# Forgetting attention in two passes: high and low halves of the queries stacked, keys held twice, values side by side

## The chip, the cores and the metric

The kernel runs on one core of a Trainium2 chip. The metric is the device time of one execution in microseconds. TensorE multiplies, with the stationary operand loaded by its own instruction; ScalarE, VectorE and GpSimd do the elementwise work; SyncE and ScalarE issue DMAs here.

## The reference, cut to what matters

A decoder layer of four sub-layers for 512 tokens of width 1024: a SwiGLU, a mixer (forgetting attention with 8 heads of 64 beside gated linear attention), a cross-attention to 256 memory tokens, and a second SwiGLU. All is float32. The part that the change touches:

```python
def fox_attention(q, k, v, log_f):
    c = jnp.cumsum(log_f, axis=1).transpose(0, 2, 1)
    ...
        s = jnp.einsum('bhqd,bhkd->bhqk', qi, kt).astype(jnp.float32) * scale
        s = s + ci[..., None] - c[:, :, None, :]
        s = jnp.where(k_pos[None, :] <= q_pos[:, None], s, -jnp.inf)
        p = jax.nn.softmax(s, axis=-1).astype(vt.dtype)
        return jnp.einsum('bhqk,bhkd->bhqd', p, vt)
```

with 8 heads, 64 wide, and queries taken in blocks of 128.

## The kernel before

Float32 products are made from float32r parts. Each operand x is kept as a rounded high part (ScalarE, a copy into float32r) and a low part, x minus high (VectorE, or GpSimd for the weights), and a product is three passes of TensorE: high by high, low by high, high by low (`three`).

Weights stream in blocks of 128x1024 through four slots. SyncE fetches a block in two pieces of 256 KB (`fetch`, L493), ScalarE rounds it into w_hi (`round_block`, L644), GpSimd subtracts it into w_lo (`split`, L588), TensorE uses it and frees the slot. The order on every engine is written out by hand; each engine works its own queue in order, and semaphores tie the queues together.

**The mixer's projections** take four blocks each: queries (group 0), keys (1), values (2), and then the linear attention's groups 3 to 5. `in_evacuate` takes a group out of the banks. For queries and keys VectorE scales a bank into tmp (L1282, one row block m holds two heads of 64 rows), ScalarE rounds, VectorE subtracts. A head's queries lie in their own head slot of q_hi and q_lo, 64 rows of them, and the other 64 rows of the slot are zero: `three` contracts over 128 rows, two heads of keys, and the zero rows drop the head that is not wanted. GpSimd clears those rows once (L626), in its queue between the low halves of the mixer's third and fourth block. Keys are kept two heads to a row block (k_hi_a, k_hi_b, k_lo), values with all heads beside each other (v_hi, v_lo).

ScalarE's order from the keys to the heads' loop is: round keys of heads 0 to 3 (`in_evacuate(1, (0, 1))`), a weight block, the first decays, a weight block, `cum_spread(0)` (which needs TensorE's `cum_rows(0)`, L1678, made right ahead of the last value block), the second decays, keys of heads 4 to 7, values of the first two token blocks, a weight block, the other values, and then the loop. TensorE's wait ahead of the loop is for the low halves of queries and keys and for the clearing.

**The loop over heads** (`fox_attention` on each engine) has 32 units, 8 heads by 4 query blocks. For a unit k TensorE makes the mask product (L1701) and the three score products (`scores`), then `fill(k)`, one or two quarters of a block of groups 3 to 5 as the table FILL says, then, for the third unit after a head's last, the head's output (`output`), and then the transposes of unit k-2 (`turn`, L1713). VectorE takes maxima (L1165) and normalises; ScalarE takes exponentials (L851) and rounds the transposed probabilities (pt_hi, L861), and VectorE makes their low half (pt_lo, L1178). The output product has 128 columns of values, two heads, as stationary operand, so half of the rows of bank 3 are not used. ScalarE rounds the head's 64 rows into fox_hi (L842), and VectorE subtracts into fox_lo (L1152). Behind the loop comes `gla`, where TensorE waits for the last of these, runs a warm-up product (L1445), and then the first scores of the linear attention, which wait for ScalarE's two copies of the turned keys (L916).

## Time and profile before

| | us |
|---|---|
| median of 3 runs | 1189.07 (1186.98 to 1190.51) |
| the profiled execution | 1188.42 |
| its span | 1186.7 |
| TensorE busy in the span | 1160.1 |
| mean granted clock | 0.998 |

A span runs from the first to the last instruction of the profiled execution. The time of that execution is 1.7 us more than its span, for what lies around it. Matmuls are pipelined: the duration that is printed for one of them overlaps the next, so what a product costs is read from where the next one starts. The mixer's projections begin at about 375 us, the loop over heads runs from 452.7 to about 571.7 us.

### The profile page before, as it was taken

Reading aid. Unit: us, or ns where it says so; the run is one execution under the profiler, and the core shown is the slowest. Engines: PE = TensorE matmul, PEld = TensorE weight load, DVE = VectorE, ACT = ScalarE, POOL = GpSimd, SP = SyncE. Lnnn points to the kernel's source line nnn. Section 1 sums busy time; section 2 is a strip of 40 time slices with the busy share of each in tenths; the row PEclk is TensorE's granted clock in tenths of the full one; section 3 lists DMA queues with packets and bytes.
Section 4 is the critical chain, followed back from the end, with each engine's and each line's share of the span. In section 5 each row is a group of like instructions: output and inputs, shape, how many; then the busy total and the mean of one; then the engine's idle time right before and its main releaser. Section 6 shows DMA issues by size and latency. Waiting matters only on the chain.

```text
span 1186.7 us, 15254 instructions
## 1 busy us (share of the span) xinstructions
PE 1160.1 (98%) x5664; PEld 965.5 (81%) x5664; DVE 352.4 (30%) x718; ACT 454.6 (38%) x744; POOL 499.4 (42%) x227
## 2 busy tenths in 40 slices
PE   8999999999999999999899999899999999999998
PEld 7888888888888778787778988778888888888886
DVE  2221311310006274655545204544122131130003
ACT  6232332322126455454535545456423233231213
POOL 5354354354443542222325754256434435435441
PEclk9999999999999999999999999999999999999999
DMA  6323333332322222111223442233332333323232
GB/s 201 105 91 99 96 94 101 92 103 89 106 89 71 89 89 72 54 54 43 83 69 109 160 142 89 73 126 107 104 105 90 98 96 92 103 89 106 89 107 107
DMA packets 86141, 115.13 MB, mean 97 GB/s; under 512 B 8974, under 2 KB 54092, under 8 KB 86092
## 3 DMA queue, kind: packets, MB, share of 16 engines
q1 hardware_dynamic: 86000, 114.44, 29.7%
q8 instruction: 33, 0.54, 0.2%
q14 instruction: 16, 0.13, 0.0%
q10 hardware_dynamic: 92, 0.02, 0.0%
HBM read 112.34 MB, written 2.10 MB: 96 GB/s over the span
## 4 chain that ended last, share of the span: by engine, by line
PE 61%; issue 24%; POOL 11%; DVE 2%; DMA 1%; ACT 1%; POOLq 0%; SPq 0%; DVEq 0%
PE bank L1436 20%; PE bank L1440 20%; PE bank L1437 20%; POOL w_lo L588 10%; PE bank L1477 1%; DVE h L1073 1%; DMA raw<-in_ffn_w_gu 1%; DVE bank L1062 0%; PE bank L1513 0%; POOL q_hi L626 0%; POOL q_lo L626 0%; DVE tmp L1062 0%; DVE f_ms L1060 0%; ACT w_hi L644 0%; ACT xh L658 0%
## 5 line engine op out<-in xcount | busy, mean ns | idle before, releaser
L588 POOL TENSOR_TENSOR w_lo<-raw,w_hi 128x1024 fp32r<-128x1024 f32 x204 | 488.3, 2403 | 665.0 <-ACT w_hi L644 664.3
L1436 PE MATMUL bank<-xh,w_hi 128*128 128x512 f32 (+1 forms) x912 | 349.8, 384 | 2.7 <-POOL w_lo L588 2.0
L1437 PE MATMUL bank<-xh,w_lo 128*128 128x512 f32 (+1 forms) x912 | 348.3, 382 | 0.0
L1440 PE MATMUL bank<-xl,w_hi 128*128 128x512 f32 (+1 forms) x912 | 348.3, 382 | 0.0
L644 ACT ACTIVATE w_hi<-raw 128x1024 fp32r<-128x1024 f32 x204 | 213.3, 1057 | 349.5 <-DMA raw<-in_ffn_w_down 167.5
L1436 PEld LDWEIGHTS bank<-xh,w_hi 128*128 128x128 f32 x912 | 171.5, 188 | 36.6 <-POOL w_lo L588 2.6
L1440 PEld LDWEIGHTS bank<-xl,w_hi 128*128 128x128 f32 x912 | 171.4, 188 | 33.6
L1437 PEld LDWEIGHTS bank<-xh,w_lo 128*128 128x128 f32 x912 | 171.5, 188 | 32.0
L1436 PE MATMUL bank<-w_hi,mid_hi 128*128 128x512 f32 x352 | 137.3, 390 | 0.0
L1440 PE MATMUL bank<-w_lo,mid_hi 128*128 128x512 f32 x352 | 137.0, 389 | 0.0
L1437 PE MATMUL bank<-w_hi,mid_lo 128*128 128x512 f32 x352 | 136.9, 389 | 0.0
L1107 DVE TENSOR_TENSOR tmp<-bank,rinv 128x512 f32<-128x512 f32 x44 | 30.2, 686 | 343.8 <-PE bank L1440 327.6
L753 ACT ACTIVATE tmp<-tmp 128x512 f32<-128x512 f32 x44 | 27.8, 633 | 152.0 <-DVE tmp L1107 152.0
L1436 PEld LDWEIGHTS bank<-w_hi,mid_hi 128*128 128x128 f32 x352 | 66.1, 188 | 14.1 <-DVE tmp L1108 0.6
L1440 PEld LDWEIGHTS bank<-w_lo,mid_hi 128*128 128x128 f32 x352 | 66.1, 188 | 13.9
L1437 PEld LDWEIGHTS bank<-w_hi,mid_lo 128*128 128x128 f32 x352 | 66.1, 188 | 13.6
L1436 PE MATMUL bank<-w_hi,xh 128*128 128x512 f32 x160 | 64.6, 404 | 3.3 <-POOL w_lo L588 2.9
L1440 PE MATMUL bank<-w_lo,xh 128*128 128x512 f32 x160 | 63.0, 394 | 0.0
L1437 PE MATMUL bank<-w_hi,xl 128*128 128x512 f32 x160 | 63.0, 394 | 0.0
L1062 DVE SCALAR_TENSOR_TENSOR bank<-bank,g_row 128x512 f32<-128x512 f32 x20 | 13.7, 693 | 135.4 <-ACT sq L691 135.4
L1062 DVE SCALAR_TENSOR_TENSOR tmp<-bank,g_row 128x512 f32<-128x512 f32 x12 | 8.1, 684 | 105.8 <-ACT sq L691 105.8
L1436 PEld LDWEIGHTS bank<-w_hi,xh 128*128 128x128 f32 x160 | 30.5, 190 | 10.4 <-issue 4.1
(232 smaller groups left out, 1211.6 us busy)
## 6 DMA issues: line engine op xcount, KB each, us to landing
raw<-in_ffn_w_gu SPq DMA_DIRECT2D x176, 256.0 KB, 2.9
raw<-in_ffn_w_down SPq DMA_DIRECT2D x88, 256.0 KB, 2.8
raw<-in_mix_w_in SPq DMA_DIRECT2D x48, 256.0 KB, 2.8
raw<-in_mem_w_kv SPq DMA_DIRECT2D x32, 256.0 KB, 3.1
raw<-in_mem_w_o SPq DMA_DIRECT2D x32, 256.0 KB, 2.9
raw<-in_mix_w_out SPq DMA_DIRECT2D x16, 256.0 KB, 3.0
raw<-in_mem_w_q SPq DMA_DIRECT2D x16, 256.0 KB, 2.9
h<-in_x SPq DMA_DIRECT2D x4, 512.0 KB, 5.3
```

The lines of the kernel that those rows point to most:

```text
L588: gp.tensor_tensor(w_lo[:, n % SLOTS, :], raw[:, n % SLOTS, :], w_hi[:, n % SLOTS, :].bitcast(F32), ALU.subtract).then_inc(lo_ready, 1)
L644: act.activation(w_hi[:, n % SLOTS, :], raw[:, n % SLOTS, :], ACT.Copy).then_inc(hi_ready, 1)
L753: act.activation(tmp[:, pair, :], tmp[:, pair, :], ACT.Silu).then_inc(silu_done, 1)
L1062: dve.scalar_tensor_tensor(out=weighted_at(n)[:, :], in0=out_bank(s, n)[:, :], scalar=POST_SCALE[s], in1=g_row[:, cols], op0=ALU.mult, op1 ...
L1073: dve.scalar_tensor_tensor(out=h[:, t, cols], in0=weighted_at(n)[:, :], scalar=f_rinv[:, r], in1=h[:, t, cols], op0=ALU.mult, op1=ALU.add) ...
L1107: dve.tensor_tensor(tmp[:, pair, :], b[pair][:, :], rinv[:, :], ALU.mult).then_inc(gate_scaled, 1)
L1436: pe.matmul(dst, w[0], x[0], start=start, stop=False, skip_group_check=loose)
L1437: pe.matmul(dst, w[1], x[0], start=False, stop=False, skip_group_check=loose)
L1440: return pe.matmul(dst, w[0], x[1], start=False, stop=stop, skip_group_check=loose)
L1477: last = pe.matmul(bank[m][:, TOK[half]], slot[:, cols], x[:, c, TOK[half]], start=half == c == 0 and not low_w and not low_x, stop=False, ...
```

## The change

The queries of a head are stacked along the contraction: the head's slot of q_hl has its high part in its own 64 rows and its low part in the other 64. The keys of each head are held twice, once in each half of the rows, so that one pass with k_hi gives high by high and low by high, and a pass with k_lo gives high by low and also low by low. The second copy of the keys is made by DMA, from one half of the rows to the other, 8 for k_hi and 8 for k_lo, issued by ScalarE. Of the values of a head the high and the low part lie side by side as 128 stationary columns (v_hl), so that two passes, with pt_hi and pt_lo, fill both halves of bank 3: one with the product of the high part, one with that of the low part. ScalarE copies one half out, VectorE adds the other, and high and low part of the sum are made one unit later. The clearing of the q tiles is gone. The diff, cut:

```diff
-            gp.wait_ge(w_used, B_IN)
-            gp.wait_ge(lo_ready, B_IN + 3)
-            for n, t in enumerate((q_hi, q_lo)):
-                for e in range(2):
...
-                    gp.memset(heads[:, :, e, :].bitcast(F32), 0.0).then_inc(q_zero, 1)
@@ ScalarE, in_evacuate @@
                     elif g == 1:
                         act.wait_ge(in_tmp, 4 + m + 1)
-                        act.activation(key_hi(m), tmp[:, m, :], ACT.Copy).then_inc(in_hi, 1)
+                        for e, done in enumerate((k_even_hi, in_hi)):
+                            r = head_rows(e)
+                            act.activation(k_hi[r, 2 * m + e, :], tmp[r, m, :], ACT.Copy).then_inc(done, 1)
+                        for e, (done, count) in enumerate(((k_even_hi, m + 1), (in_hi, 4 + m + 1))):
+                            act.wait_ge(done, count)
+                            act.dma_start(k_hi[head_rows(e + 1), 2 * m + e, :].bitcast(F32),
+                                          k_hi[head_rows(e), 2 * m + e, :].bitcast(F32))\
+                               .then_inc(k_hi_twin[m // 2], 16)
...
+            def low_twins(half):
+
+                for m in (2 * half, 2 * half + 1):
+                    for e, (done, count) in enumerate(((k_even_lo, m + 1), (in_lo, 4 + m + 1 + 4 * half))):
+                        act.wait_ge(done, count)
+                        dst = key_lo(2 * m + e)
+                        act.dma_start(dst[head_rows(e + 1), :].bitcast(F32),
+                                      dst[head_rows(e), :].bitcast(F32)).then_inc(k_lo_twin[half], 16)
@@ ScalarE, fox_attention @@
-                    r = slice(FOX_D * (hd % 2), FOX_D * (hd % 2 + 1))
-                    act.activation(fox_hi[r, hd // 2, :], bank[3][r, :], ACT.Copy).then_inc(y_h, 1)
+                    r, other = fox_rows_of(hd), fox_rows_of(hd + 1)
+                    act.activation(fox_y[r, hd // 2, :], bank[3][other, :], ACT.Copy).then_inc(y_part, 1)
+
+                def round_rows(done):
...
+                    act.wait_ge(y_sum, hd + 1)
+                    act.activation(fox_hi[r, hd // 2, :], fox_y[r, hd // 2, :], ACT.Copy).then_inc(y_h, 1)
 
                 for k in range(N_FOX + LATE + 2):
+                    if k == 4:
+                        low_twins(1)
...
                     output(k - LATE - 1)
+                    round_rows(k - LATE - 2)
@@ ScalarE, mixer @@
                 in_evacuate(2, (0, 1))
+                low_twins(0)
                 round_to(B_IN + KB * 3 + 2)
@@ VectorE, fox_attention @@
+                    dve.wait_ge(y_part, hd + 1)
+                    dve.tensor_tensor(fox_y[r, c, :], bank[3][r, :], fox_y[r, c, :],
+                                      ALU.add).then_inc(y_sum, 1)
+
+                def low_rows(done):
...
                     dve.wait_ge(y_h, hd + 1)
-                    dve.tensor_tensor(fox_lo[r, c, :], bank[3][r, :], fox_hi[r, c, :].bitcast(F32),
+                    dve.tensor_tensor(fox_lo[r, c, :], fox_y[r, c, :], fox_hi[r, c, :].bitcast(F32),
                                       ALU.subtract).then_inc(y_l, 1)
@@ TensorE, scores @@
-                        pe.wait_ge(in_lo, 12)
+                        pe.wait_ge(k_hi_twin[1], 16 * 4)
+                        pe.wait_ge(k_lo_twin[1], 16 * 4)
...
-                    three(dst, (q_hi[:, hd, tok], q_lo[:, hd, tok]), (key_hi(c)[:, 0:w], k_lo[:, c, 0:w]),
-                          False, True, True).then_inc(scored, 1)
+                    pe.matmul(dst, q_hl[:, hd, tok], k_hi[:, hd, 0:w], start=False, stop=False, skip_group_check=True)
+                    pe.matmul(dst, q_hl[:, hd, tok], key_lo(hd)[:, 0:w], start=False, stop=True,
+                              skip_group_check=True).then_inc(scored, 1)
@@ TensorE, output @@
-                        last = three(bank[3][:, q0:SEQ],
-                                     (v_hi[:, j, c * P:(c + 1) * P], v_lo[:, j, c * P:(c + 1) * P]),
-                                     (pt_hi[:, j, q0:SEQ], pt_lo[:, j, q0:SEQ]), j == 0, j == TC - 1, True)
+                        q0 = min(j, 2) * P
+                        for pt in (pt_hi, pt_lo):
+                            last = pe.matmul(bank[3][:, q0:SEQ], v_hl[:, j, hd, :], pt[:, j, q0:SEQ],
+                                             start=j == 0 and pt is pt_hi, stop=j == TC - 1 and pt is pt_lo,
+                                             skip_group_check=True)
@@ TensorE, mixer @@
-                pe.wait_ge(in_lo, 6)
+                pe.wait_ge(in_lo, 4)
                 pe.wait_ge(q_even_lo, 4)
-                pe.wait_ge(q_zero, 4)
+                pe.wait_ge(k_hi_twin[0], 16 * 4)
+                pe.wait_ge(k_lo_twin[0], 16 * 4)
                 fox_attention()
```

ScalarE's queue before, from the second decays (L818, L819) to the first exponential of the loop. Here k_hi_b is the keys of heads 4 to 7, and the w_hi row is a weight block.

```order
L831 ACTIVATE cum_b<-bank 128x512 [waits cb_done]
L818 ACTIVATE gke<-gke 128x1024
L819 ACTIVATE gk<-gb 128x1024
L805 ACTIVATE k_hi_b<-tmp 128x512 [waits in_tmp,exps]
L805 ACTIVATE k_hi_b<-tmp 128x512 [waits in_tmp]
L809 ACTIVATE v_hi<-bank,rinv_tok 128x512 [waits hinv,pair_done] x2
L644 ACTIVATE w_hi<-raw 128x1024 [waits landed3]
L809 ACTIVATE v_hi<-bank,rinv_tok 128x512 [waits hinv,w_used] x2
```

The same stretch of ScalarE's queue with the change, from the keys of heads 4 to 7 to the weight block.

```order
L817 ACTIVATE k_hi<-tmp 64x512 [waits in_tmp,exps]
L817 ACTIVATE k_hi<-tmp 64x512
L820 DMA k_hi<-k_hi 64x512 [waits k_even_hi]
L820 DMA k_hi<-k_hi 64x512 [waits in_hi]
L817 ACTIVATE k_hi<-tmp 64x512 [waits in_tmp]
L817 ACTIVATE k_hi<-tmp 64x512
L820 DMA k_hi<-k_hi 64x512 [waits k_even_hi]
L820 DMA k_hi<-k_hi 64x512 [waits in_hi]
L829 ACTIVATE v_hl<-bank,rinv_tok 128x8x64 [waits hinv,pair_done] x2
L840 DMA k_lo_a<-k_lo_a 64x512 [waits k_even_lo]
L840 DMA k_lo_a<-k_lo_a 64x512 [waits in_lo]
```

Two further DMAs, for the low keys of heads 2 and 3, follow there. Two operations on keys became four with four DMAs, each DMA behind a wait for the operation that made its source; the same happened to the keys of heads 0 to 3 earlier in the queue. The four DMAs of low keys stand ahead of the weight block and of the loop.

TensorE's queue before, at the first two units of the loop; the mask product is L1701.

```order
L1701 MATMUL bank<-causal,ident_r 128x256 [waits q_zero,q_even_lo,in_lo]
L1436 MATMUL bank<-k_hi_a,q_hi 128x256
L1437 MATMUL bank<-k_hi_a,q_lo 128x256
L1440 MATMUL bank<-k_lo,q_hi 128x256
L1701 MATMUL bank<-causal,ident_r 128x256 [waits cb_ready]
```

TensorE's queue with the change, at the same place.

```order
L1759 MATMUL bank<-causal,ident_r 128x256 [waits k_hi_twin0,k_lo_twin0,q_even_lo,in_lo]
L1762 MATMUL bank<-k_hi,q_hl 128x256
L1763 MATMUL bank<-k_lo_a,q_hl 128x256
L1759 MATMUL bank<-causal,ident_r 128x256 [waits cb_ready]
L1762 MATMUL bank<-k_hi,q_hl 128x256
```

One score product per unit is gone, and the first mask product waits for the keys' copies in place of the clearing.

## Rows read from the trace of the kernel before

**Rows 1.** The page's first part: busy time, share of the span, instructions of TensorE.

```profile
PE 1160.1 (98%) x5664; PEld 965.5 (81%) x5664; DVE 352.4 (30%) x718; ACT 454.6 (38%) x744; POOL 499.4 (42%) x227
```

**Rows 2.** Timeline of TensorE in the loop: start, us, engine, line, operation.

```profile
506.67 0.28 PE L1436 MATMUL bank<-k_hi_b,q_hi 128*128 128x256 f32 x1
506.79 0.28 PE L1437 MATMUL bank<-k_hi_b,q_lo 128*128 128x256 f32 x1
506.90 0.28 PE L1440 MATMUL bank<-k_lo,q_hi 128*128 128x256 f32 x1
...
515.01 0.39 PE L1436 MATMUL bank<-pt_hi,v_hi 128*128 128x512 f32 x1
515.23 0.39 PE L1437 MATMUL bank<-pt_hi,v_lo 128*128 128x512 f32 x1
515.46 0.39 PE L1440 MATMUL bank<-pt_lo,v_hi 128*128 128x512 f32 x1
```

**Rows 3.** Timeline at the mixer's fourth weight block, GpSimd and TensorE.

```profile
384.84 3.66 POOL L626 MEMSET q_hi<- 64x2048 f32 x2
388.56 3.67 POOL L626 MEMSET q_lo<- 64x2048 f32 x2
...
394.75 0.50 PE L1436 MATMUL bank<-xh,w_hi 128*128 128x512 f32 x1 [1.11 <-POOL w_lo L588]
```

**Rows 4.** Timeline from the first keys to the loop's first product.

```profile
441.00 1.23 ACT L805 ACTIVATE k_hi_a<-tmp 128x512 fp32r<-128x512 f32 x2 [7.01 <-DVE tmp L1282]
...
442.13 1.05 ACT L644 ACTIVATE w_hi<-raw 128x1024 fp32r<-128x1024 f32 x1
...
447.03 0.40 PE L1678 MATMUL bank<-cum_hl,sel 128*128 128x512 f32 x1
447.22 0.80 SPq L493 DMA_DIRECT2D raw<-in_mix_w_in  x2
...
447.46 0.60 ACT L831 ACTIVATE cum_b<-bank 128x512 f32<-128x512 f32 x1 [0.84 <-PE bank L1678]
...
449.98 1.15 ACT L805 ACTIVATE k_hi_b<-tmp 128x512 fp32r<-128x512 f32 x2
...
451.04 1.25 ACT L809 ACTIVATE v_hi<-bank,rinv_tok 128x512 fp32r<-128x512 f32 x2
...
452.18 1.05 ACT L644 ACTIVATE w_hi<-raw 128x1024 fp32r<-128x1024 f32 x1
...
452.71 0.28 PE L1701 MATMUL bank<-causal,ident_r 128*128 128x256 f32 x1
```

**Rows 5.** Operations of 64 rows on a q tile: count, min/median/max ns, first and last start.

```profile
L802 ACT ACTIVATE q_hi<-tmp x8: 629/631/633, 409.7 to 414.3; 64x512 fp32r<-64x512 f32 x8
...
L1152 DVE TENSOR_TENSOR q_lo<-bank,q_hi x8: 682/688/695, 473.5 to 572.5; 64x512 fp32r<-64x512 f32 x8
```

**Rows 6.** DMA issues: count, KB each, median us from issue to landing.

```profile
raw<-in_mix_w_in SPq DMA_DIRECT2D x48, 256.0 KB, 2.8
...
out<-h SPq DMA_DIRECT2D x8, 256.0 KB, 2.0
```

**Rows 7.** Waits from 370 to 640 us: us in total, times, longest us.

```profile
DVE pt_lo L1178 <- ACT pt_hi L861: 46.1, 26, 3.5
...
PE bank L1713 <- DVE pt_lo L1178: 2.5, 4, 1.0
...
PE bank L1436 <- DVE pt_lo L1178: 2.0, 2, 1.4
```

**Rows 8.** Timeline behind the last head.

```profile
572.53 1.09 ACT L916 ACTIVATE gla_a<-bank 128x512 f32<-128x512 f32 x2
...
574.35 0.72 PE L1839 MATMUL bank<-gq,gk 64*128 64x128 f32 x8
```

**Rows 9.** Windows: PE, PEld, DVE, ACT, POOL busy, then granted clock, DMA share, GB/s.

```profile
746.00:748.00 2.00, 0.38 (x3) 0.38 (x4) 0.86 (x2) 1.11 (x2) 1.09 (x1) 1.00 0.00 0
750.00:752.50 2.50, 2.50 (x8) 1.95 (x7) 0.69 (x1) 0.59 (x3) 0.00 (x0) 0.50 0.00 0
```

**Rows 10.** Timeline of TensorE inside and behind that dip.

```profile
750.06 0.63 PE L1440 MATMUL bank<-w_lo,xh 128*128 128x512 f32 x1
750.49 0.63 PE L1436 MATMUL bank<-w_hi,xh 128*128 128x512 f32 x1
...
753.04 0.39 PE L1436 MATMUL bank<-w_hi,xh 128*128 128x512 f32 x1
753.27 0.39 PE L1437 MATMUL bank<-w_hi,xl 128*128 128x512 f32 x1
```

More of the change, by code:

```diff
@@ L284, in build @@
         reset = sb("reset", [P, SEQ], at=shared + 100 * kib)
-        fox_hi, fox_lo = (t[:, :, :].rearrange("p (c e) n -> p c e n", e=2)[:, :, 0, :] for t in (q_hi, q_lo))
+        fox_hi, fox_lo = (t[:, :, :].rearrange("p (c e) n -> p c e n", e=2)[:, :, 0, :] for t in (q_hl, k_hi))
+        q_flat = sb("q_flat", [P, FOX_H, SEQ], at=shared + 16 * kib)
+        fox_y = q_flat[:, :, :].rearrange("p (c e) n -> p c e n", e=2)[:, :, 0, :]
         gla_o = sb("gla_o", [P, GLA_H, 2, SEQ], at=shared)
@@ L357, in build @@
         in_tmp = sem("in_tmp")
-        q_zero = sem("q_zero")
+        k_even_hi = sem("k_even_hi")
+        k_even_lo = sem("k_even_lo")
+        k_hi_twin = [sem(f"k_hi_twin{i}") for i in range(2)]
+        k_lo_twin = [sem(f"k_lo_twin{i}") for i in range(2)]
         q_even_hi = sem("q_even_hi")
@@ L376, in build @@
         y_l = sem("y_l")
+        y_part = sem("y_part")
+        y_sum = sem("y_sum")
         ke_turned = sem("ke_turned")
@@ L446, in wait_group, with fox_rows_of, head_rows, key_lo @@
                 eng.wait_ge(w_used, B_IN + KB * (g + 1))
-        def key_hi(c):
-            return (k_hi_a, k_hi_b)[c // 2][:, c % 2, :]
+        def fox_rows_of(hd):
+            return slice(FOX_D * (hd % 2), FOX_D * (hd % 2 + 1))
+        def head_rows(e):
+            return slice(FOX_D * (e % 2), FOX_D * (e % 2 + 1))
+        def key_lo(hd):
+            if hd < 2:
+                return k_lo_a[:, hd, :]
+            return k_lo_b[:, hd - 2, :] if hd < 6 else k_lo_c[:, hd - 6, :]
         def fox_slot(u):
@@ L1182, in fox_attention @@
                     output(k - LATE - 1)
+                    low_rows(k - LATE - 2)
                     for g in (3, 5):
```

66 lines of the change are left out of this document (39 added, 27 removed).

## The prediction

> **What bounds the kernel now.** I began with the page's busy shares. TensorE is busy for 98% of the span [rows 1], so this change is priced in TensorE time first: by the time between the starts of two products, since the printed durations of one product overlap the next. In the heads' stage a 512-column product follows the last after 0.23 us, a 256-column one after 0.12 us [rows 2]; taking 0.17 us for 384 columns is the value between them. Then I looked, stretch by stretch, for places where TensorE waits although the share says 98%, because there work taken from TensorE may come back as a longer wait. There are three kinds. Before the mixer's fourth weight block TensorE waits 1.11 us for GpSimd, which has just been clearing the q tiles [rows 3]. Inside the heads' stage it waits for VectorE's low halves, in ones and twos of a microsecond. At the stage's start it does not wait at all today: the first product of the heads starts at 452.71 [rows 4], right behind the last value product. That last place is where I expect the change to be decided, since all that the heads now need is made there by ScalarE.
>
> **Part 1: products removed.** A unit's scores were three products after the mask, and are two. The moving widths of a head's four units are 256, 256, 384 and 512, so one product fewer per unit saves 0.12 + 0.12 + 0.17 + 0.23 = 0.64 us a head. The output was three products for each of four key blocks (512, 384, 256 and 256 columns) and is two: 0.64 us again. Over 8 heads that is 16 x 0.64 = 10.2 us [rows 2]. All of it lies on TensorE's own queue. Where VectorE already holds TensorE up, part may be lost; I book that in part 4. The pitch of the 256-column products is not held up by the weight load, or 256 columns would not take half of what 512 take.
>
> **Part 2: the clearing of the q tiles goes.** GpSimd cleared four half tiles from 384.84 to 392.23 (3.66 and 3.67 us for two each), then made the low half of the fourth block, and TensorE waited 1.11 us for it [rows 3]. With the clearing gone that low half can start as soon as ScalarE has rounded the block, more than two microseconds earlier, and nothing else is late there: -1.1 us.
>
> **Part 3: the keys' copies delay the first scores.** TensorE now waits, before its first score, for four copies of k_hi and four of k_lo. Follow ScalarE's queue, in the times of the profile before. (a) Keys of heads 0 to 3: two operations of 128 rows started at 441.00, and the next operation at 442.13 [rows 4], 1.13 us. Now there are four of 64 rows, and 64 rows cost as much as 128: 0.63 us each [rows 5]. After each pair ScalarE waits for its own end and then issues two DMAs. The nearest price of an issue is SyncE's, 0.80 us for two pieces [rows 4]. So a pair costs about 1.3 + 0.8 = 2.1 us and both 4.1 us, 3.0 us more than before. (b) What follows is unchanged and was nearly back to back: cum_b started at 447.46 after 0.84 us of idle time, so 3.0 - 0.84 = 2.1 us arrive there. (c) Keys of heads 4 to 7: started at 449.98, now 452.1, and again 4.1 us instead of 1.06: 456.2. (d) The two v_hi operations, 1.14 us by their starts [rows 4]: 457.4. (e) Four more issues at 0.4 us: the last one starts at 458.6. (f) Its landing. No SBUF to SBUF copy is in this trace. The nearest rows are the output pieces, 256 KB in 2.0 us, and the weight pieces, 256 KB in 2.8 us [rows 6]; a copy here is 64 rows x 2 KB = 128 KB and reads no HBM, so I take 2.0 with some queueing, 2.3. TensorE starts at 460.9 instead of 452.7: +8.2 us. Ends: 5.5 us (issues as cheap as nothing, landing 2.0) and 9.5 us (landing 2.8, waits between the pairs). A second stall lies inside this one and costs nothing more: the block rounded at 442.13 comes 3.0 us later, its low half ends at about 449 where TensorE wants it at 447.3, but TensorE then only reaches the same wait later.
>
> By the Trainium skill (DMA: Bandwidth & Descriptors, Rules for kernel authors) transfers to disjoint partition halves serialize, since both use the same engines. The copies are such halves; their ScalarE issues are spaced 0.4 us apart anyway, so by that rule the sum would move by less than the range of (f). No row here shows two of them together.
>
> **Part 4: more work for ScalarE and VectorE in the heads' loop.** Each head's output was one ScalarE copy (rounding) and one VectorE subtraction. Now ScalarE copies the other half out of the bank, VectorE adds, ScalarE rounds one unit later, VectorE subtracts: one 64-row operation more on each, 0.63 and 0.69 us [rows 5]. VectorE's stands, in its queue, before the maximum of the next head's first unit, and TensorE's transposes are behind that. Further, the low keys of heads 4 to 7 are four 64-row subtractions instead of two of 128 rows (+1.4 us on VectorE at unit 2), and ScalarE issues four DMAs before the exponential of unit 4 (+1.6 us there). If all of it reached TensorE it would be 7 x 0.69 + 1.4 + 1.6 = 7.8 us, if none 0. Most of it is covered: in the mixer VectorE stood idle 46.1 us before its low halves of the probabilities, waiting for ScalarE, and TensorE waited for those low halves only 4.5 us in six places [rows 7], four of them (2.5 us) before the transposes. I price the added operation in full at those four and halve it, since VectorE has idle time of its own beside them: 4 x 0.69 / 2 = 1.4 us, and 0.7 us for units 2 to 4: +2.1 us, ends 0 and 6.
>
> **Part 5: the way into the linear attention.** ScalarE's two copies of the turned keys follow the last head's output. They started at 572.53 and took 1.09 us; TensorE's first score product there was at 574.35, with the copies done at 573.6 [rows 8]. Now VectorE's addition (0.69) and ScalarE's rounding (0.63) come first, so the copies end at about 575.0: +0.7 us, ends 0 and 1.4. TensorE's own wait ahead of its warm-up products keeps its length, as it now waits for the addition where it waited for the subtraction.
>
> **Part 6: the clock.** The trace holds one dip: after a stretch of 2 us in which TensorE was busy 0.38 us, the granted clock read 0.50 (1.2 GHz) [rows 9], and 512-column products followed each other after 0.43 us instead of 0.23 [rows 10]; some seven products were hit, about 1.6 us. The stall of part 3 is an idle stretch of some 7 us, far longer than the one before that dip, so I expect another dip whose end lies in the first scores: +1.6 us, ends 0 and 3.4 (if it lasts over twice as many products). By the Trainium skill (TensorE: Matmul & The Clock Gate, the part on the HAM clock gate) the array falls to 1.2 GHz when idle and only sustained activity brings it back. The row agrees with that (0.50 right behind the idle stretch), and the rule speaks against this change: by it the sum below holds at +1.3 us, and if one dip in a whole execution were chance it would be -0.3 us.
>
> **The sum.** -10.2 - 1.1 + 8.2 + 2.1 + 0.7 + 1.6 = +1.3 us, against the profiled execution's 1188.4 us (span 1186.7): 1189.7. The median of the runs is 0.65 us above that execution, which gives **1190.4 us**. A measurement of this kernel can tell about 0.3%, or 3.6 us, from no change, so the forecast is "within 0.3%".
>
> **The rivals.** *A: the copies are in time.* If issuing and landing cost next to nothing on the way, or ScalarE's chain has slack that I don't see, the stall of part 3 stays under 2 us and brings no dip: -10.2 - 1.1 + 1.5 + 2.1 + 0.7 = -7.0, or 1182. For it: nothing but the cheapness of small DMA issues. Against it: ScalarE stands in line from 447.46 on with no gap [rows 4]. Chance 0.17, with the milder forms (a stall of 4 us, 1185) in it. *B, slower: the clock.* The stall splits TensorE's work, the clock stays at 1.2 GHz through the stall and twice as long behind it (3.3 us), and falls a second time at the longer pause of part 5 (1.6 us). The point from which it decides is a clock still at 0.50 well behind the first scores, when the low stretch covers over some ten 512-column products. With the loop's 2.1 us grown to 3.5: 1.3 + 1.7 + 1.6 + 1.4 = +6.0, or 1195. For it: one dip behind 2 us of near idleness. Against it: VectorE and ScalarE get ahead while TensorE runs slowly, which shortens later waits. Chance 0.33 for a time over 1192.6, all mixtures counted. *C: the products don't shrink as planned*, since a stage limited by VectorE's and ScalarE's loop gives nothing back when TensorE gets faster: part 1 shrinks to some 7 us, +4.5, or 1193.6; TensorE's long busy stretches in the stage speak against it. It is in B's chance with 0.08.
>
> **How the numbers follow.** Forecast (within 0.3%) 0.48; faster 0.19 (A, and a little for a part 3 at its lower end); slower 0.33. The range takes in A's milder part and B: 1183.5 to 1196. A full A (1182) and both B and C together lie outside.
>
> **What the changed profile would show.** Part 1: 512-column products at 0.23 us with two per unit, and a heads' stage about 10 us shorter in TensorE products. Part 2: no wait on GpSimd before the fourth block. Part 3: TensorE idle for about 7 us ahead of the first mask product, released by a DMA into k_lo, with ScalarE's queue full in the 12 us ahead. Part 6: a granted clock of 0.50 right behind it. I would be wrong if that stall is under 4 us (then faster), if TensorE's waits for low halves in the loop more than double, or if copies land in over 3 us.

## The result and the profile after

| | before | after |
|---|---|---|
| median, us | 1188.83 (5 runs, 1186.98 to 1190.51) | 1200.49 (5 runs, 1199.59 to 1201.25) |
| span of the profiled execution | 1186.7 | 1197.4 |
| mean granted clock | 0.998 | 0.996 |
| first mask product of the heads | 452.71 | 460.49 |
| from there to the transposes behind the last head | 119.0 | 124.2 |

The ratio is 1.0098, with an interval of 1.0085 to 1.0111: the changed kernel is 11.7 us slower. The forecast was 1190.4 and its range ended at 1196.0, so both were missed, on the slow side.

The page of the changed kernel opens with the same line as [rows 1].

```profile
span 1197.4 us, 15161 instructions
## 1 busy us (share of the span) xinstructions
PE 1152.5 (96%) x5600; PEld 957.0 (80%) x5600; DVE 364.4 (30%) x730; ACT 462.9 (39%) x756; POOL 492.1 (41%) x223
```

TensorE has 64 products fewer and is busy 7.6 us less, in a span that is 10.7 us longer. So some 18 us of new time lie in its pauses. The largest of them stand among its waits (us in total, times, longest us) from 450 to 600 us; the first two rows are to be read beside [rows 7].

```profile
PE bank L1772 <- DVE pt_lo L1229: 12.2, 11, 1.9
PE bank L1759 <- DMA k_lo_b<-k_lo_b: 7.0, 1, 7.0
PE bank L1789 <- DVE pt_lo L1229: 2.2, 2, 1.4
PE bank L1493 <- DVE tmp L1335: 1.7, 2, 1.4
```

The second row is the stall that the prediction spoke of. The first is the one that it did not: the transposes (L1772) wait for VectorE's low halves 11 times and 12.2 us, where they waited 4 times and 2.5 us. The wait ahead of the output products (L1789) is what it was.

**The stall.** ScalarE's queue between the keys of heads 4 to 7 and the loop, where [rows 4] showed two operations of 128 rows and no gap (start, us, engine, line, operation):

```profile
451.06 1.29 ACT L817 ACTIVATE k_hi<-tmp 64x512 fp32r<-64x512 f32 x2
451.72 1.12 ACTq L820 DMA_DIRECT2D k_hi<-k_hi  x2
452.89 1.28 ACT L817 ACTIVATE k_hi<-tmp 64x512 fp32r<-64x512 f32 x2 [0.55 <-ACT k_hi L817]
453.55 1.12 ACTq L820 DMA_DIRECT2D k_hi<-k_hi  x2
454.77 0.69 ACT L829 ACTIVATE v_hl<-bank,rinv_tok 128x512 fp32r<-128x512 f32 x1 [0.60 <-ACT k_hi L817]
...
455.39 0.61 ACTq L840 DMA_DIRECT2D k_lo_a<-k_lo_a  x1
456.04 1.28 ACTq L840 DMA_DIRECT2D k_lo_b<-k_lo_b  x2
```

and TensorE at the end of it:

```profile
453.06 0.39 PE L1497 MATMUL bank<-w_lo,xh 128*128 128x512 f32 x1
460.49 0.55 PE L1759 MATMUL bank<-causal,ident_r 128*128 128x256 f32 x1 [7.04 <-DMA k_lo_b<-k_lo_b]
```

The last value product starts at 453.06, and the copy issued last, near 456.7, releases TensorE at 460.49. The landings are longer than I took them (KB each, median us from issue to landing):

```profile
k_hi<-k_hi ACTq DMA_DIRECT2D x8, 128.0 KB, 3.7
...
k_lo_b<-k_lo_b ACTq DMA_DIRECT2D x4, 128.0 KB, 3.0
```

**The clock.** Windows as in [rows 9]; the granted clock is the figure behind POOL's.

```profile
454.00:456.00 2.00, 0.00 (x0) 0.00 (x0) 0.51 (x1) 1.40 (x3) 0.00 (x0) 1.00 0.76 188
458.00:460.00 2.00, 0.00 (x0) 0.00 (x0) 0.00 (x0) 1.57 (x3) 1.51 (x1) 0.50 0.65 168
462.00:464.00 2.00, 2.00 (x6) 1.56 (x6) 1.83 (x6) 0.83 (x4) 0.00 (x0) 0.50 0.00 0
467.00:468.00 1.00, 1.00 (x6) 0.79 (x6) 0.94 (x3) 0.00 (x0) 0.00 (x0) 1.00 0.00 0
```

The clock falls to 1.2 GHz within the stall and is there for 10.2 us in all, from 456.3 to 466.5. TensorE works in the last 6.1 of them, at half its speed, which costs some 3.0 us.

**The loop.** I counted TensorE's timeline row by row from the first mask product to the transposes behind the last head: the products at the pitch of [rows 2], the waits over 0.25 us, and what is left (short gaps and slow clock).

| us | before | after | |
|---|---|---|---|
| products at full pitch | 106.9 | 96.7 | -10.2 |
| waits over 0.25 us | 6.9 | 19.9 | +13.0 |
| short gaps, slow clock | 5.3 | 7.5 | +2.2 |
| the loop | 119.0 | 124.2 | +5.2 |

So 7.8 us come from the later start (0.7 of them were already lost in the first 10 us of this execution, ahead of everything that the change touches), 5.2 from the loop and 0.7 from the way into the linear attention, together 13.7; 3.0 of them are given back later: the dip of [rows 9] does not occur (1.5 us), and about as much is gained at the hand-over to the last SwiGLU.

**What VectorE meets in the loop.** Here GpSimd, VectorE and TensorE stand around one head's output, cut from the timeline; q_flat is the sum in SBUF, and the operation on `k_hi<-q_flat,q_hl` is the subtraction that makes the sum's low half (L1203), which is kept in the place of k_hi and goes by that name.

```profile
519.36 2.39 POOL L605 TENSOR_TENSOR w_lo<-raw,w_hi 128x1024 fp32r<-128x1024 f32 x1 [10.74 <-ACT w_hi L654]
...
520.10 2.19 DVE L1203 TENSOR_TENSOR k_hi<-q_flat,q_hl 64x512 fp32r<-64x512 f32 x1
...
522.21 0.27 DVE L1216 CUSTOM_DVE_ANT_0 prob<-bank,cum_b 128x128 f32<-128x128 f32 x1
...
523.43 0.56 DVE L1229 TENSOR_TENSOR pt_lo<-bank,pt_hi 128x384 fp32r<-128x384 f32 x1 [0.34 <-ACT pt_hi L900]
...
524.13 0.63 PE L1772 MATMUL bank<-ident,prob 128*128 128x128 f32 x4 [1.74 <-DVE pt_lo L1229]
```

The subtraction takes 2.19 us and ends 0.54 us behind GpSimd's operation on the weights; the maximum behind it (L1216), the low half and the transposes are late by it. Over the eight heads (min/median/max ns):

```profile
L1203 DVE TENSOR_TENSOR k_hi<-q_flat,q_hl x8: 684/1370/2186, 487.8 to 586.9; 64x512 fp32r<-64x512 f32 x8
```

Two kinds lie behind that median. Four of the eight begin while GpSimd makes a low half of the weights and take 2.05 to 2.19 us; the other four run with GpSimd idle and take 0.68 to 0.69. In [rows 5] the eight subtractions of the same shape took 682 to 695 ns. One thing that differs is the operand: before, one of the two inputs was bank 3; now both are in SBUF. The other is the time: before, none of the eight ran beside a GpSimd operation. Run a2 tells the two apart.

### The profile page after: what moved, and what is told of

It is laid out like the page before. It is cut to its first block, busy times and chain, and to the rows that moved or that the text cites. A ratio compares the mean times of both kernels' runs of the same rounds, so it can differ in the third digit from the quotient of the medians.

```text
span 1197.4 us, 15161 instructions
## 1 busy us (share of the span) xinstructions
PE 1152.5 (96%) x5600; PEld 957.0 (80%) x5600; DVE 364.4 (30%) x730; ACT 462.9 (39%) x756; POOL 492.1 (41%) x223
## 4 chain that ended last, share of the span: by engine, by line
PE 61%; issue 25%; POOL 10%; DVE 2%; DMA 1%; ACT 0%; POOLq 0%; SPq 0%; DVEq 0%
PE bank L1493 20%; PE bank L1497 20%; PE bank L1494 20%; POOL w_lo L605 10%; PE bank L1534 1%; DVE h L1114 1%; DMA raw<-in_ffn_w_gu 1%; PE bank L1570 0%; DVE bank L1103 0%; DVE tmp L1103 0%; DMA raw<-in_mix_w_in 0%; DVE f_ms L1101 0%; ACT w_hi L654 0%; ACT sq L701 0%; PE bank L1555 0%
```

## The experiments

Three causes were open: the stall (how it arises, and what it costs with the clock behind it), the slow subtraction, and whether TensorE's saved products are worth their time at all in this loop. For each run the table gives the ratio to the kernel before on the same chip, the start of the loop, its length and, by the same count as above, its waits and its rest. The runs stand in the order of the sections below.

| run | ratio [interval] | start | loop | waits, rest |
|---|---|---|---|---|
| after | 1.0098 [1.0085, 1.0111] | 460.5 | 124.2 | 19.9, 7.5 |
| a1 low copies early | 1.0088 [1.0070, 1.0107] | 455.0 | 127.5 | 24.3, 6.5 |
| a2 sum in PSUM | 1.0056 [1.0039, 1.0074] | 460.3 | 118.1 | 14.9, 6.4 |
| a3 copies by SyncE | 1.0027 [1.0015, 1.0039] | 452.3 | 122.2 | 19.5, 6.0 |
| a4 both | 0.9992 [0.9982, 1.0001] | 452.4 | 117.2 | 15.3, 5.0 |
| b1 scores alone | 1.0067 [1.0050, 1.0084] | 460.5 | 120.8 | 11.3, 7.5 |
| b2 b1, copies by SyncE | 0.9995 [0.9985, 1.0004] | 452.0 | 118.7 | 11.8, 5.2 |
| b3 outputs alone | 1.0041 [1.0027, 1.0055] | 453.2 | 122.3 | 15.4, 5.1 |
| b4 b3, sum in PSUM | 0.9997 [0.9988, 1.0007] | 453.7 | 117.3 | 10.4, 5.2 |
| c1 a4, passes put back | 1.0037 [1.0026, 1.0049] | 452.3 | 123.8 | 10.8, 6.1 |
| c2 a4, FILL moved | 0.9949 [0.9930, 0.9969] | 451.6 | 112.8 | 9.6, 6.5 |
| c3 a4, half of the sum | 0.9940 [0.9918, 0.9962] | 452.0 | 114.1 | 12.2, 5.2 |
| c4 a4, values first | 1.0000 [0.9990, 1.0011] | 452.3 | 118.7 | 15.5, 6.5 |
| d1 before, FILL moved | 0.9975 [0.9965, 0.9984] | 453.6 | 116.3 | 3.9, 5.5 |
| d2 after, FILL moved | 1.0047 [1.0030, 1.0063] | 460.2 | 115.4 | 10.4, 8.2 |

The ratio is from several executions, the other columns are from one profile each. Where a short gap counts as a wait is a choice that moves up to 0.6 us between the last two numbers. A profile can also hold a stretch of low clock that the next execution has not: those of a3, c1, c2, c4 and d2 have one of 3.4 us inside the loop behind its first units, which costs up to 1.7 us there, a4's has none.

### a1: the low copies of heads 0 to 3 issued earlier

The last copies to land are those of k_lo, issued behind the first two value operations. This run issues them ahead of the decays.

```diff
                 round_to(B_IN + KB * 3)
+                low_twins(0)
                 decays(0)
...
                 in_evacuate(2, (0, 1))
-                low_twins(0)
```

> One edit on the changed kernel: the four DMAs that copy the low keys of heads 0 to 3 are issued by ScalarE before the first decays, not behind the first two value operations. Theory S (start): of the 11.7 us lost against before, some 7 us are TensorE's idle stretch ahead of the first mask product, and some 3 us the low clock that follows it. Then the copies land before TensorE arrives, the idle stretch of 7.2 us shrinks to under 4 us (what is left is ScalarE's queue, 2.5 us later for the early issues, on which the value halves and maxima of the first units hang), and the time falls by 3 to 6 us, to 1195 to 1197.5. Rival L (loop): the loss is the loop's waits for the low halves of the probabilities (12.2 us against 2.5 before), and the start is made up for later: then the time stays within 1.5 us of 1200.5.

The first mask product starts at 454.96, 5.5 us earlier (7.2 us by the work, as this execution lost 1.7 us more in its first 40 us), but the loop grows from 124.2 to 127.5, and the run's ratio is within the interval of after. Most of the stall has only moved: the first products of the linear attention's groups, which need the value banks free, now wait for VectorE's v_hl.

```profile
PE bank L1493 <- DVE v_hl L1354: 4.4, 1, 4.4
```

What makes TensorE wait is ScalarE's queue as a whole, not the place of the last copies in it: the values, too, are late by the key operations and the issues ahead of them. The low stretch of the clock at the loop's start shrinks from 10.2 to 3.4 us.

### a2: the sum stays in PSUM

VectorE adds into bank 3, ScalarE rounds from there, and the subtraction has one operand in PSUM again. The next head's output products wait for the subtraction instead of the addition.

```diff
-                    dve.tensor_tensor(fox_y[r, c, :], bank[3][r, :], fox_y[r, c, :],
+                    dve.tensor_tensor(bank[3][r, :], bank[3][r, :], fox_y[r, c, :],
...
-                    dve.tensor_tensor(fox_lo[r, c, :], fox_y[r, c, :], fox_hi[r, c, :].bitcast(F32),
+                    dve.tensor_tensor(fox_lo[r, c, :], bank[3][r, :], fox_hi[r, c, :].bitcast(F32),
```

> One edit on the changed kernel: VectorE writes the sum of a head's two halves back into PSUM bank 3 and not into SBUF, so that its later subtraction reads one operand from PSUM, as before the change; TensorE's next output waits for that subtraction. Number and size of the operations are the same. Theory P (port): the subtraction with both operands in SBUF waits for GpSimd's weight split (0.68 to 2.19 us, median 1.37, where before it was 0.69 always). Then all eight read 0.69 us, TensorE's waits for the low halves of the probabilities fall from 14 us by 3 to 6, and the time by 3 to 5 us, to about 1196.5. Rival C (chain): the added operations lengthen ScalarE's and VectorE's chain whatever they read: then the subtraction is short, but the time is within 1 us of 1200.5.

Three views of this run: the eight subtractions, one of them in the timeline beside GpSimd, and the transposes' wait.

```profile
L1203 DVE TENSOR_TENSOR k_hi<-bank,q_hl x8: 682/688/694, 486.6 to 580.6; 64x512 fp32r<-64x512 f32 x8
```

```profile
517.28 2.38 POOL L605 TENSOR_TENSOR w_lo<-raw,w_hi 128x1024 fp32r<-128x1024 f32 x1 [10.73 <-ACT w_hi L654]
...
517.98 0.68 DVE L1203 TENSOR_TENSOR k_hi<-bank,q_hl 64x512 fp32r<-64x512 f32 x1
```

```profile
PE bank L1772 <- DVE pt_lo L1229: 7.6, 10, 1.3
```

Again four of the eight begin 0.7 to 0.8 us into a GpSimd operation, at the same heads, and all eight take 0.68 to 0.69 us. The transposes wait 4.6 us less, and the ratio falls from 1.0098 to 1.0056, some 5 us. (The clock's low stretch is 6.8 us here instead of 10.2, with a stall of the same length, and TensorE works in 3.7 us of it instead of 6.1, so some 1.2 of the 5 us are the clock's.) So neither the operand's place nor GpSimd alone makes a subtraction long: it takes both inputs in SBUF and a GpSimd operation beside it. By the Trainium skill (SBUF — State Buffer, the section on SBUF's two separate sides), VectorE and GpSimd share one pair of ports as an exclusive lock; a VectorE operation with two SBUF inputs contends for it with a GpSimd operation that reads SBUF, and the loser is blocked until the other ends. The rows agree with that: the subtraction at 520.10 began 0.74 us into a GpSimd operation of 2.39 us and ended 0.54 us after it, and with one input in PSUM none was longer than 0.694 us.

### a3 and a4: SyncE issues the copies; and both repairs

In a3 all 16 copies are issued by SyncE, between its weight fetches, behind the same waits; ScalarE keeps its 64-row operations. a4 is a3 with a2's edit.

```diff
             for n in range(B_IN, B_OUT):
                 fetch(n, row_pair(a["mix_w_in"][0], (n - B_IN) % KB, IN_COLS[(n - B_IN) // KB]))
+                if n == B_IN + 13:
+                    high_twins(0)
+                    low_twins(0)
+                if n == B_IN + 15:
+                    high_twins(1)
+                if n == B_IN + 16:
+                    low_twins(1)
```

> One part of the changed kernel moved: all sixteen copies of the keys are issued by SyncE, between its weight fetches, and ScalarE issues none and waits for none of its own operations. Theory S: ScalarE's queue is then only 0.1 to 1.3 us longer per pair of row blocks than before the change, TensorE's idle stretch ahead of the loop is under 2 us, no clock dip follows, and the time falls by 9 to 11 us, to about 1190.5. If the copies' landing (2.2 to 4.4 us in the changed kernel) and not ScalarE's queue sets the start, 3 us of idle time remain and the time is about 1194. Rival L: under 4 us are gained, since the loop's waits are what is left.

> Both edits together: copies issued by SyncE, and the sum of the halves kept in PSUM. If the start and the port collision are separate causes, the gains add: 1200.5 less 10 less 4, about 1186.5, which is below the 1188.8 of before. If the loop is bound by the length of ScalarE's and VectorE's chain, the second edit gives nothing beside the first, and the time is that of the run with copies by SyncE within 1 us.

In a3 the copies that the loop's start needs are away before the value products are even done, TensorE goes into the loop without a pause, and the clock stays at 2.4 GHz there (a short dip, 3.4 us, comes later, at 494). SyncE's issues, then TensorE's first products of the loop:

```profile
441.94 2.46 SPq L569 DMA_DIRECT2D k_hi<-k_hi  x4
...
445.72 1.90 SPq L577 DMA_DIRECT2D k_lo_b<-k_lo_b  x2
```

```profile
452.02 0.39 PE L1502 MATMUL bank<-w_lo,xh 128*128 128x512 f32 x1
452.25 0.28 PE L1764 MATMUL bank<-causal,ident_r 128*128 128x256 f32 x1
```

The ratio falls from 1.0098 to 1.0027, 8.4 us: that is what it costs to let ScalarE wait for its own results and issue the copies, with the clock's part in it. The waits in the loop are the same (19.5 against 19.9). The move has one side effect: the last of the four low-key subtractions of heads 0 to 3, which also has both inputs in SBUF, now begins 0.05 us into a GpSimd operation of 2.41 us and takes 2.90 us instead of 0.69. Its copy still lands in time.

```profile
L1355 DVE TENSOR_TENSOR k_lo_b<-tmp,k_hi x4: 676/687/2901, 443.5 to 459.1; 64x512 fp32r<-64x512 f32 x4
```

In a4 the waits are 15.3 and the ratio is 0.9992: both repairs together bring the change back to no difference, 12.6 us for the two where they gave 8.4 and 5.0 one by one. Still, the products save 10.2 us here as well, a4's profile has neither stall nor dip, and 9.3 of those us are missing. A small part may be the clock's: the granted clock of a4's ten executions is 0.997 in the median, that of the kernel before on the same chip 0.998, which is some 1 us.

### b1 to b4: each half of the change alone

b1 keeps only the stacked scores and has the old outputs; b2 is b1 with the copies issued by SyncE. b3 keeps only the values side by side, with the old scores and the clearing; b4 is b3 with the sum in PSUM. Each saves 5.1 us of products. The core of b1 and of b3 as they differ from the changed kernel:

```diff
-                        for pt in (pt_hi, pt_lo):
-                            last = pe.matmul(bank[3][:, q0:SEQ], v_hl[:, j, hd, :], pt[:, j, q0:SEQ],
+                        last = three(bank[3][:, q0:SEQ],
+                                     (v_hi[:, j, c * P:(c + 1) * P], v_lo[:, j, c * P:(c + 1) * P]),
+                                     (pt_hi[:, j, q0:SEQ], pt_lo[:, j, q0:SEQ]), j == 0, j == TC - 1, True)
```

```diff
-                    pe.matmul(dst, q_hl[:, hd, tok], k_hi[:, hd, 0:w], start=False, stop=False, skip_group_check=True)
-                    pe.matmul(dst, q_hl[:, hd, tok], key_lo(hd)[:, 0:w], start=False, stop=True,
-                              skip_group_check=True).then_inc(scored, 1)
+                    three(dst, (q_hi[:, hd, tok], q_lo[:, hd, tok]), (key_hi(c)[:, 0:w], k_lo[:, c, 0:w]),
+                          False, True, True).then_inc(scored, 1)
```

> The scores' half of the change alone (queries stacked, keys twice, copies issued by ScalarE; output products, values and their two operations per head as before). By the theory so far: -5.1 us of products and -1.1 us of clearing, against +7.8 us at the start of the loop and 2 to 3 us of low clock behind it, in sum 4 to 6 us slower than before, ratio about 1.004. Rival L (the loop's longer chain carries the loss): no slower than before, since the added operations per head are gone.

> The scores' half alone with the copies issued by SyncE. Theory: -5.1 - 1.1 us, against 1.9 us of waiting for the value halves at the first fill and about 1 us in the loop: 3 to 4 us faster than before, ratio about 0.997. If the removed products are not worth their pitch, because VectorE's and ScalarE's chain fills what they leave, the ratio is 0.999 to 1.001.

> The output's half of the change alone, on the kernel before (values side by side, two passes per key block, sum of the halves in SBUF, the added operation on ScalarE and on VectorE). Theory P (port): -5.1 us of products, +4 to 5 us from VectorE's subtraction behind GpSimd's splits, +1.3 us at the linear attention: within 1.5 us of before, ratio 1.000. Rival C (chain length): the same or slower, and the next kernel no better than this one.

> As the run of the outputs alone, with the sum of the halves kept in PSUM. Theory P: 3 to 5 us less than that run, ratio about 0.9965 against before. Rival C: within 1 us of that run.

b1 against b2 prices ScalarE's copies a second time, 8.6 us; b3 against b4 prices the sum in SBUF again, 5.2 us. In b3 the slow subtraction is there with no copies and no stall in the kernel:

```profile
L1182 DVE TENSOR_TENSOR q_lo<-q_flat,q_hi x8: 683/1374/2199, 477.5 to 577.7; 64x512 fp32r<-64x512 f32 x8
```

b2 and b4 are each free of the flaw of their half, each saves 5.1 us of products, and neither is faster than before: 0.9995 and 0.9997. Before had 6.9 us of waits in the loop; b2 has 11.8 and b4 10.4. In b2 nothing was added to any engine in the middle of the loop but two subtractions and SyncE's issues. Of its 4.9 us of new waits 1.8 do come from an addition, ahead of the loop: TensorE waits for the value halves at the first fill, since ScalarE now makes four key operations (2.6 us) before them where it made two. For the other 3 us the only added work in the loop is the two subtractions (1.4 us of VectorE's time); most of it looks like the saving turned into waits, which c1 tests.

### c1 and c3: where the rest of the gain went

c1 takes a4 and makes the low-key pass and the low-probability pass twice, which puts the removed products back on TensorE and changes nothing else; those two terms count double in what it computes. c3 takes a4 and leaves out the other half of each head's sum: no copy by ScalarE, no addition by VectorE, and the rounding goes back one unit earlier.

```diff
                     pe.matmul(dst, q_hl[:, hd, tok], k_hi[:, hd, 0:w], start=False, stop=False, skip_group_check=True)
+                    pe.matmul(dst, q_hl[:, hd, tok], key_lo(hd)[:, 0:w], start=False, stop=False, skip_group_check=True)
...
-                        for pt in (pt_hi, pt_lo):
+                        for n, pt in enumerate((pt_hi, pt_lo, pt_lo)):
```

```diff
-                    r, other = fox_rows_of(hd), fox_rows_of(hd + 1)
-                    act.activation(fox_y[r, hd // 2, :], bank[3][other, :], ACT.Copy).then_inc(y_part, 1)
...
-                    dve.wait_ge(y_part, hd + 1)
-                    dve.tensor_tensor(bank[3][r, :], bank[3][r, :], fox_y[r, c, :],
-                                      ALU.add).then_inc(y_sum, 1)
```

> On the kernel with copies by SyncE and the sum in PSUM: each unit's pass with the low keys and each key block's pass with the low probabilities is made twice, so that TensorE has all its 10.2 us of products back and nothing else changes (the scores and outputs count those terms twice). Theory F (the loop's turns are set by VectorE's and ScalarE's chain, so a shorter TensorE only waits longer): most of the 10.2 us disappears in waits of the loop, which fall from 15.3 us to about 9, and the time rises by 3 to 6 us only, to 1190 to 1192. Rival W (the added operations make the waits, whatever TensorE does): the waits stay at 15 us and the time rises by 9 to 10 us, to 1196.

> On the kernel with copies by SyncE and the sum in PSUM: only one half of bank 3 is taken out (ScalarE rounds it, VectorE subtracts, as before the change), so the copy, the addition and the late turn are gone while TensorE's two passes stay. The output leaves out half of every head's sum. Theory F: the waits fall little, from 15.3 us to 12 or more, 1 to 3 us in the time. Rival W: they fall to 9 or less, and the time is under 1182.

c1 is 1.0037 against a4's 0.9992: 10.2 us of products put back cost 5.3 us (6.6 by the two loops, with a low stretch of the clock in c1's alone). So with this loop's order the removal is worth only about half of itself, since TensorE then arrives earlier where it waits for VectorE. The transposes' wait shows it, c1 first and then a4:

```profile
PE bank L1778 <- DVE pt_lo L1234: 3.3, 7, 0.8
```

```profile
PE bank L1777 <- DVE pt_lo L1234: 6.3, 9, 1.2
```

c3 is 0.9940: by the ratios the added copy, addition and later rounding cost 6.2 us in a4, by the two profiles' loops 3.1 (117.2 to 114.1); I had priced them at 1.4. A part of the difference is the choice of execution: a4's profile is its fastest of ten, 1.4 us under its median, and c3's its slowest of four, 1.5 us over its median. The two causes are not independent, so 4.9 us lost on the products and 3 to 6 us for the added operations are no exact split of the 9.3.

### c2, d1 and d2: the fill moved to where TensorE waits

TensorE's fill between scores and transposes is the table FILL. It had two quarters in the third unit of every head. Now, in every head but the first, one of them is in the head's first unit, where the moving width is 256 and TensorE comes to the transposes soonest; the 48 quarters are the same.

```diff
-FILL = (0, 1, 2, 2, 1, 1, 2, 2, 1, 1, 2, 1,
-        1, 1, 2, 2, 1, 1, 2, 2, 1, 1, 2,
-        1, 1, 1, 2, 1, 1, 1, 2, 2, 2, 2)
+FILL = (0, 1, 2, 2, 2, 1, 1, 2, 2, 1, 1, 1, 2, 1, 1, 2, 2, 1, 1, 2, 2, 1, 1, 1, 2, 1, 1, 1, 2, 1, 1, 2, 2, 2)
```

> On the kernel with copies by SyncE and the sum in PSUM: the table FILL gives the first unit of each head two quarters and takes one from the third or fourth, 48 in all as before. The waits of the loop lie at the first two units of a head, where one quarter (1.4 us of products) stands beside the chain. Theory F: with two quarters there the waits fall by 2 to 4 us, if the other units can spare one: time 1183 to 1185. Rival: the waits move to the units that lost a quarter, and the time is within 1 us of 1186.5.

> The kernel before with the moved FILL table alone. If the first units of a head are where the loop's chain sticks out in any version, the waits of 6.9 us there fall by about 2 us and the time with them, ratio about 0.998. If the moved table only pays once TensorE's products are fewer (Theory F: the cover got too thin through the change), the ratio is 0.9995 to 1.001, and the 5 us that it brought beside the repaired change belong to the change.

> The changed kernel with the moved FILL table alone (copies by ScalarE, sum in SBUF). The stall at the start and the low clock stay (8 us and some 4 us); the loop's waits fall by 5 to 8 us, since two quarters also cover part of VectorE's wait for GpSimd's split: 1193 to 1195. If the port collision is what waits there, and no cover helps, it stays above 1197.

c2 (on a4) is 0.9949, 1181.67 us, the fastest complete kernel of the study. Of its waits from 452 to 590 us the largest no longer is that of the transposes:

```profile
PE bank L1496 <- DVE tmp L1338: 2.7, 1, 2.7
PE bank L1792 <- DVE pt_lo L1232: 2.3, 4, 1.4
PE bank L1496 <- DVE v_hl L1357: 1.8, 1, 1.8
```

The table alone, on the kernel before, gives 0.9975 (3.0 us), on a4 it gives 5.1 us, and on the changed kernel as it was 6.1 (1.0098 to 1.0047). Between before and a4 the sign fits the account, since with shorter products the place of the cover should be worth more. The 6.1 are not the cover's alone, as the last row of this section shows. With the table moved in both, the repaired change is worth 0.9949 against 0.9975, some 3 us. The intervals of these two touch (0.9969 and 0.9965), so of that 3 us the sign is likely and the size is not settled. The waits in d2's loop are 10.4 us, against 19.9 in the changed kernel. But the table also moved VectorE against GpSimd: only two of d2's eight subtractions (2.18 and 2.21 us) still meet a GpSimd operation, where four did.

```profile
L1201 DVE TENSOR_TENSOR k_hi<-q_flat,q_hl x8: 683/689/2207, 485.5 to 577.8; 64x512 fp32r<-64x512 f32 x8
```

### c4: values ahead of the second keys

In a4 TensorE waits 1.7 us for v_hl behind its first scores. c4 evacuates the first values ahead of the keys of heads 4 to 7.

```diff
-                in_evacuate(1, (2, 3))
                 in_evacuate(2, (0, 1))
+                in_evacuate(1, (2, 3))
```

> On the kernel with copies by SyncE and the sum in PSUM: ScalarE takes out the first two value blocks ahead of the keys of heads 4 to 7. TensorE's 1.7 us of waiting for the value halves at the first fill goes or falls under 0.5 us, and the time by 1 to 1.5 us, to about 1185.3; if the loop's chain only resumes later, the time stays within 0.5 us of 1186.5.

The wait that c4 was made for is gone; another has come in its place. First a4's wait, then c4's TensorE and ScalarE:

```profile
454.99 0.47 PE L1498 MATMUL bank<-xh,w_hi 128*128 128x512 f32 x1 [1.73 <-DVE v_hl L1359]
```

```profile
452.84 0.28 PE L1768 MATMUL bank<-k_lo_a,q_hl 128*128 128x256 f32 x1
452.96 0.40 PE L1498 MATMUL bank<-xh,w_hi 128*128 128x512 f32 x1
...
453.74 1.06 ACT L676 ACTIVATE w_hi<-raw 128x1024 fp32r<-128x1024 f32 x1
454.71 1.24 ACT L846 ACTIVATE v_hl<-bank,rinv_tok 128x512 fp32r<-128x512 f32 x2
...
456.96 0.48 PE L1498 MATMUL bank<-xh,w_hi 128*128 128x512 f32 x1 [1.99 <-DVE v_hl L1359]
```

TensorE goes from its first scores into the fill without a pause. It then comes to the next fill, which needs the other two token blocks' values out of their banks, 2.1 us earlier than in a4, and waits there 2.0 us: ScalarE rounds those values behind the weight block, at 454.71 in c4 and 454.81 in a4. So the keys of heads 4 to 7 did make the first values late, and the loop's start gains nothing by it as long as the last values stand where they do. The ratio is 1.0000 against 0.9992, with intervals that overlap; c4's profile also has a low stretch of the clock from 457.3 on, right behind that wait. Values of all four blocks ahead of the weight block were not tried.

## Why the prediction was wrong

**Part 1, the products: right in amount, wrong in worth.** TensorE's products shrank by 10.2 us exactly. The step that failed was that all of it lies on TensorE's own queue and is worth its full amount there. I left the loss to part 4, which priced only the added operations; nowhere did I price that TensorE, with one product fewer in each unit and four fewer in each head's output, would reach the same low halves earlier. c1 shows that this takes 4.9 of the 10.2 in the repaired kernel. It was rival C, which I gave 0.08 and dismissed with TensorE's long busy stretches. But those stretches were only as long as the products in them, and the 2.5 us in four places of [rows 7] said that the slack to VectorE was already used up in some units.

**Part 4, the loop: the term that was mis-sized.** It read +2.1 with ends 0 and 6. The waits grew by 13.0. The shares that the runs price are these: the subtraction with both operands in SBUF, 4 to 5 us (four of them 1.4 to 1.5 us longer), which no step of mine had (I took a VectorE operation to cost what its shape costs, wherever its operands are); the added operations and the later rounding, 3 to 6 us by c3, where halving the four waits of [rows 7] gave 1.4; and part 1's lost share. My own sign of failure, "if TensorE's waits for low halves in the loop more than double", is what happened: 4.5 us to 14.4 (12.2 and 2.2).

**Part 2, the clearing: right.** TensorE was 0.7 us behind the kernel before when it came to the mixer's fourth weight block, and 0.7 us ahead of it behind that block, where it no longer waits for GpSimd: 1.4 us instead of 1.1. The 0.7 us behind are from the first 10 us of the kernel, which no edit touches: the same product of the first SwiGLU starts at 36.65 in the profile of before, at 37.34 in that of after, and between 36.71 and 39.05 in those of the other runs. That is a difference between executions, and no term of the sum.

**Part 3, the stall: right in kind, and in its number by luck.** Predicted 8.2 us; measured 8.5, from 0.7 us ahead of the kernel before to a start at 460.49, 7.8 behind it. Two errors offset each other. ScalarE's chain was shorter than in my steps: a pair of keys took 1.85 us instead of 2.1, and the last copy was issued near 456.7, which is 457.4 in the times of before, instead of 458.6. From there to TensorE's start it was 3.8 us where I had 2.3. The prediction's warning sign, "if copies land in over 3 us", was met for k_hi (3.7). a3 and b2 confirm the cause by removing it. That another issuing queue could have avoided the stall I did not see.

**Part 5: right.** From ScalarE's copies of the turned keys the prediction had +0.7; the first linear-attention products stand 3.34 us behind the last head's transposes instead of 2.63, +0.7.

**Part 6, the clock: right in kind, low in size.** One dip behind the stall, as said, with 6.1 us of work at half speed, about 3.0 us instead of 1.6 and inside the upper end of 3.4. The dip of [rows 9], which I had used as the measure of its length, is a low stretch of 3.4 us from 749.1 on; this one is three times as long, behind a far longer pause. Rival B foresaw this much of it; its second dip did not come.

**The sum.** Predicted +1.3; the loop term alone was -6.5 (parts 1, 4 and 6) and came out at +5.2, 11.7 us worse; the stall, the clearing and the way out of the loop came to 7.8 (8.5 - 1.4 + 0.7), as predicted; 0.7 us was the slower beginning, and 3.0 us came back behind the loop, which leaves the 9.4 us between the forecast's +1.3 and the measured +10.7. The range went wrong because its slow end was rival B alone. The loop that gives half of the saving back was rival C, which I had put outside the range together with B; the operation that GpSimd holds up was in no term and no rival; and both push the same way.

## What to carry to other kernels

Where two engines take turns, removing work from the one that looks busiest pays only as far as the other's results are already there: count the waits in that stretch first, and when the products go, move the cover to the unit whose wait grows (here that gave 3.0 us on the kernel before and 5.1 on the repaired one). Before an operand moves from PSUM to SBUF, look which GpSimd operations run beside that VectorE operation. And a DMA that an engine must issue behind its own result costs that engine's queue the wait and the issue; a queue with nothing urgent behind it can carry the same copies. Here that gave 8.4 us.

## What the runs showed of the hardware

- A VectorE subtraction of 64x512 with both inputs in SBUF took 2.05 to 2.19 us where it began inside one of GpSimd's weight subtractions, 0.68 to 0.69 where GpSimd was idle, and 0.68 to 0.69 in both places with one input in PSUM (a2). The low keys' subtractions, also with both inputs in SBUF, took 0.67 to 0.69 where none ran beside them, and 2.90 where one began 0.05 us into GpSimd's (a3).
- DMA issues on ScalarE's queue cost 0.47 to 0.63 us each, against SyncE's 0.62 (four in 2.46). SBUF to SBUF copies of 128 KB landed in 3.0 and 3.7 us in the median where up to eight follow each other with weight fetches between them; from 456 to 459 us the DMA engines were busy throughout (a share of 1.03 to 1.08) and moved 270 to 320 GB/s.
- The clock fell to 1.2 GHz inside a 7 us pause, stood there for 10.2 us, and was at 2.4 GHz again by 467; in b1 it was the same. In a2 and d2, with a pause of the same length, it was 6.8 us, and where the pause was split (a1) 3.4 us. What sets the length is not settled by these runs.
